# Second attention by four heads at a time: four score banks, one output bank in halves, four buffers of transposed probabilities

## The chip, the core and the metric

The kernel is one program on one NeuronCore of a Trainium2 chip. It has five engines that run side by side and meet through semaphores: PE (TensorE, the matmuls), DVE (VectorE), ACT (ScalarE), POOL (GpSimd) and SP (SyncE, which issues most DMAs). The accumulators of the matmuls lie in PSUM, eight banks of 128 partitions x 512 floats. The metric is the device time of one execution in microseconds (us); lower is better. Times below are us unless marked otherwise.

## The reference, cut to what matters

Two transformer-like blocks follow each other on 256 tokens of width 1024. The change is in the second block. It projects the tokens once (`w_in`), does three attentions, and mixes them by gates:

```python
h = rmsnorm_2(x, norm_mix_pre[l]);  proj = h @ w_in[l]
(q_mb, k_mb, v_mb, q_sw, k_sw, v_sw, q_me, g_mb, g_sw, g_me) = jnp.split(proj, cuts, axis=-1)
o_mb = moba_attention(...)     # 8 heads of 64; 256 tokens are one block: causal, with a bias
o_sw = swa_attention(...)      # 8 heads of 64 on 2 key heads, causal, window of 128, with a sink
o_me = memory_attention(...)   # 4 heads of 128 over 256 memory tokens
merged = (sigmoid(g_mb) * (o_mb @ w_branch_moba) + sigmoid(g_sw) * (o_sw @ w_branch_swa)
          + sigmoid(g_me) * (o_me @ w_branch_mem))
```

A head is scores = q k, exp(scores + bias - max), divided by the row's sum, times v.

## The kernel before, in words

Each engine has its program written out by hand, in one fixed order; the order of the Python text is the order of the queue. Weights come as units of 1 MB. Unit u is loaded into `raw` (four slots), ACT's `split(u)` makes its high part `whi`, DVE's `split(u)` its low part `wlo` (ACT waits until PE is done with the slot), and PE does every product in three matmuls (high x high, high x low, low x high).

Heads are numbered through the program. 0 to 15 are the first block's attention, 16 to 23 are MoBA heads, 24 to 31 sliding window heads (with a sink), 32 to 35 memory heads. "Second attention" here means heads 16 to 31. A head H runs over the engines like this:

- PE `score_pair(p)` (L1425, L1428): scores of heads A = 2p and B = 2p + 1, side by side in the upper and lower 64 rows of the array, into `score_bank`: bank 2 or 3.
- DVE `row_max(H)` (L2056, L2058, for a sink L2064): adds the bias, writes the negated scores to one of the four buffers `prob4`, takes the maximum. It waits for the scores and for the transposes of head H - 4 (`s_pt`), which read the same buffer. It raises `s_Sfree`: the score bank is free.
- ACT `exps(H)` (L919, L921, for a sink L930): exponentials and row sums. Waits for `row_max(H)`.
- DVE `norm_probs(H)` (L2075 to L2079): divides by the sum. Waits for `exps(H)`.
- PE `probs_T(H)` (L1475): three 128 x 128 transposes into `pt_bank`: bank 4 or 5.
- ACT `probs_out(H)` (L939): copies them to one of two buffers `probT2`. Raises `s_ptc`.
- PE `pv_pair(p)` (L1444, L1447): probabilities times values for A and B, into `out_bank`: bank 6 or 7.
- ACT `attn_hi` (L951) and DVE `attn_lo` (L2087): one pair's output as high and low part. The latter raises `s_olo`.

PE's time between these steps is filled with sixteen gate groups, `gate_group(0)` to `gate_group(15)`: 24 matmuls of 128 x 256 each (L1129), two groups to a weight unit. Each is read out by DVE `gate_out2(k)` (L2193) and passed through tanh by ACT `gate_tanh(k)` (L1027). One turn i of the loop (eight turns) holds two heads and two groups. PE does scores of the next pair, PV of the pair before, group 2i, the six transposes of heads A and B, group 2i + 1. DVE does two `row_max` and two `norm_probs` of the next pair, `attn_lo`, `gate_out2(2i)`, a weight split, `gate_out2(2i+1)`. ACT does two `exps` of the next pair, `attn_hi`, a weight split, a tanh, two `probs_out`, a tanh. After the loop come `branch(0, 0)`, 12 matmuls, and the last PV pair, then the other `branch` groups.

Of the kernel before, what the change touches and what calls it, by code (L numbers as in the profile page):

```python
# [7 lines left out]
F32 = mybir.dt.float32  # L8
# [101 lines left out]
def bank_of(g):  # L110

    if g in (G_MLP0, G_MLP0 + 1, G_MLP1, G_MLP1 + 1, G_QMB, G_QMB + 1):
        return 4 + 2 * (g % 2)
    if G_QME <= g < G_QME + 4:
        return (1, 4, 0, 5)[g - G_QME]
    if g in [f + i for f in (G_REC[0], G_FFN) for i in range(2)]:
        return 4 + g % 2
    for b in G_BR:
        if b <= g < b + 8:
            return (1, 0, 2, 3)[(g - b) % 4]  # L120
    return g % 2 if G_G2[0] <= g < G_FFN else g % 4
# [16 lines left out]
def bass_blocks(nc, A, out):  # L138
# [57 lines left out]
    with ctx:  # L196
# [192 lines left out]
        def place_of(H):  # L389

            if H < 32:
                return prob4[:, H % 4, :], probT2[:, H % 2, :], H % 4
# [12 lines left out]

        def out_bank(H):
            return 1 if H < 16 else 6 + out_of(H) % 2

# [198 lines left out]
        def _(act):  # L607
# [325 lines left out]
            def probs_out(H):  # L933
                n = 384 if H < 32 else 512
                act.wait_ge(s_pt, H + 1)
                if H >= 2:

                    act.wait_ge(s_pv, H - 1 if H < 32 else max(H - 1, 32))
                act.activation(place_of(H)[1][:, 0:n], PS[:, pt_bank(H), 0:n], ACT.Copy).then_inc(s_ptc, 1)  # L939

            def attn_hi(H):
                if not ends_out(H):
                    return
                o = out_of(H)
# [6 lines left out]
                act.activation(X[:, k, 0, :], PS[:, out_bank(H), 0:T], ACT.Copy).then_inc(s_ohi, 1)  # L951

# [75 lines left out]

            exps(16)
            exps(17)  # L1030
            for i in range(8):
                A, B = 16 + 2 * i, 17 + 2 * i
                if i < 7:
                    exps(A + 2)
                    exps(B + 2)
                if i:
                    attn_hi(A - 1)
                split(U_G2[i // 4] + i % 4 + LEAD)
                gate_tanh(2 * i)
                probs_out(A)  # L1040
                probs_out(B)
                gate_tanh(2 * i + 1)
            split(U_BR[0] + LEAD)
            attn_hi(31)
            split(U_BR[0] + 1 + LEAD)
# [71 lines left out]
        def _(pe):  # L1117
# [313 lines left out]
            def pv_pair(p):  # L1431

                A, B = 2 * p, 2 * p + 1
                pe.wait_ge(s_ptc, B + 1)
                if p:

                    pe.wait_ge(s_olo, p if p < 8 else p - 1)
                for last in range(2):
                    for H in (A, B):
                        lo, pT = 64 * (H % 2), place_of(H)[1]  # L1440
                        c = 64 * H if H < 16 else 64 * (H - 16) if H < 24 else lo
                        v = (vtok if H < 16 else v_mb if H < 24 else v_sw)[:, last, c:c + 64]
                        if not last:
                            pe.matmul(PS[lo:lo + 64, out_bank(H), 0:T], v, pT[:, 0:T], start=True, stop=False,  # L1444
                                      skip_group_check=True)
                        else:
                            pe.matmul(PS[lo:lo + 64, out_bank(H), P:T], v, pT[:, T:T + P], start=False, stop=True,  # L1447
                                      skip_group_check=True).then_inc(s_pv, 1)
# [131 lines left out]
            ins.then_inc(s_step, 1)  # L1580
            unit_a(U_QKV + 9, G_QME)
            pe.wait_ge(s_evac, G_KSW)
            score_pair(8)
            pe.wait_ge(s_bev, B_VSW + 1)
            unit_a(U_QKV + 10, G_QME + 2)

# [25 lines left out]

            for i in range(8):
                A, B = 16 + 2 * i, 17 + 2 * i
                if i < 7:
                    score_pair(9 + i)
                if i:
                    pv_pair(7 + i)
                gate_group(2 * i)
                if i == 0:  # L1620
                    pe.wait_ge(s_evac, G_QME + 4)
                probs_T(A)
                probs_T(B)
                gate_group(2 * i + 1)

            pe.wait_ge(s_olo, 12)
            branch(0, 0)
            pv_pair(15)
            for k in range(1, 8):
# [88 lines left out]
        def _(dve):  # L1718
# [362 lines left out]
            def attn_lo(H):  # L2081
                if not ends_out(H):
                    return
                o = out_of(H)
                dve.wait_ge(s_ohi, o + 1)
                X, k = attn_dst(o)
                dve.tensor_tensor(X[:, k, 1, :], PS[:, out_bank(H), 0:T], X[:, k, 0, :].bitcast(F32), ALU.subtract)\  # L2087
                   .then_inc(s_olo, 1)
# [115 lines left out]
            dve.wait_ge(s_b2, 2)  # L2204
            row_max(16)
            row_max(17)
# [4 lines left out]
            mem_q_out(1, 1)  # L2211
            split(U_QKV + 10 + LEAD)
            for i in range(8):
                A, B = 16 + 2 * i, 17 + 2 * i
                if i < 7:
                    row_max(A + 2)
                    row_max(B + 2)
                    norm_probs(A + 2)
                    norm_probs(B + 2)
                if i:  # L2220
                    attn_lo(A - 1)
                gate_out2(2 * i)
                split(U_G2[i // 4] + i % 4 + LEAD)
                gate_out2(2 * i + 1)
            branch(0, 0)
            attn_lo(31)
            for k in range(1, 8):
# [135 lines left out]
```

## Time and profile before

| | us |
|---|---|
| median of three runs (1011.65 to 1012.15) | 1011.75 |
| the profiled execution, whole | 1011.99 |
| its span, first to last instruction | 1010.1 |
| PE busy (6251 matmuls) | 996.9 (99%) |
| DVE busy | 699.5 (69%) |
| ACT busy | 546.9 (54%) |
| share of PE in the chain of work that ended last | 92% |

The stage that the change touches starts with the first score pair at 651.46 and ends behind the last PV pair at 724.72. In the timeline a row is `start, duration, engine, line, operation, out<-in, count`; matmuls overlap their successors, and so do the others a little, so that the cost of a step is read from one row's start to the next row's start, not from the duration. A bracket at the end is idle time of the engine and what ended it.

### The profile page before, as it was taken

How to read it: one execution, taken by the hardware profiler on the slowest of the kernel's cores; microseconds unless marked ns; L12 is line 12 of the kernel's file. 1: busy time of each engine (PE TensorE's matmuls, PEld its weight loads, DVE VectorE, ACT ScalarE, POOL GpSimd, SP SyncE). 2: the span in 40 equal slices, each digit the busy share in tenths (PEclk: the TensorE clock that was granted, in tenths of full speed). 3: DMA queues.
4: the chain of work that ended last, by engine and by line, in shares of the span. 5: the costliest groups of instructions: out<-in, count | busy, mean ns of one | idle time of the engine just before them, and what ended most of it. 6: DMA issues, size and time to landing. Idle time of an engine off the chain costs nothing.

```text
span 1010.1 us, 15625 instructions
## 1 busy us (share of the span) xinstructions
PE 996.9 (99%) x6251; PEld 884.8 (88%) x6251; DVE 699.5 (69%) x1000; ACT 546.9 (54%) x803; POOL 84.4 (8%) x102
## 2 busy tenths in 40 slices
PE   9999999999999999999999999999999999999997
PEld 8997888888888867888888899999999899999996
DVE  6989666556567687675756565587665769878785
ACT  7996464444447477654444453366553466555552
POOL 2710010000002210000200000000004200000000
PEclk9999999999999999999999999999999999999999
DMA  9746585656535606575655646354545626565521
GB/s 316 243 154 216 169 314 182 198 178 205 171 121 174 243 1 221 196 248 178 199 176 197 189 139 214 125 168 126 143 150 170 222 81 209 195 198 178 193 100 42
DMA packets 120307, 180.40 MB, mean 179 GB/s; under 512 B 3145, under 2 KB 93609, under 8 KB 120249
## 3 DMA queue, kind: packets, MB, share of 16 engines
q1 hardware_dynamic: 118376, 174.10, 52.8%
q0 software_dynamic: 1536, 5.36, 1.5%
q8 instruction: 41, 0.67, 0.3%
q10 hardware_dynamic: 337, 0.13, 0.0%
q14 instruction: 17, 0.14, 0.0%
HBM read 178.48 MB, written 1.10 MB: 178 GB/s over the span
## 4 chain that ended last, share of the span: by engine, by line
PE 92%; ACT 4%; DVE 3%; issue 1%; POOL 0%; DVEq 0%; POOLq 0%; ACTq 0%
PE PS L1194 28%; PE PS L1129 28%; PE PS L1136 12%; PE PS L1138 6%; PE PS L1353 4%; PE PS L1396 2%; PE PS L1493 2%; PE PS L1182 1%; PE PS L1649 1%; PE PS L1475 1%; PE PS L1263 1%; PE PS L1444 1%; PE PS L1163 1%; PE PS L1238 1%; ACT arena L799 1%
## 5 line engine op out<-in xcount | busy, mean ns | idle before, releaser
L1747 DVE TENSOR_TENSOR wlo<-raw,whi 128x2048 fp32r<-128x2048 f32 x153 | 352.0, 2304 | 112.0 <-ACT whi L636 111.7
L636 ACT ACTIVATE whi<-raw 128x2048 fp32r<-128x2048 f32 x153 | 291.8, 1910 | 139.6 <-PE PS L1194 101.1
L1129 PE MATMUL PS<-XA,whi 128*128 128x256 f32 x1488 | 272.2, 285 | 0.0
L1129 PEld LDWEIGHTS PS<-XA,whi 128*128 128x128 f32 x1488 | 232.6, 192 | 3.0 <-issue 1.9
L1129 PE MATMUL PS<-XA,wlo 128*128 128x256 f32 x744 | 210.4, 283 | 0.0
L1194 PE MATMUL PS<-whi,XB 128*128 128x512 f32 x728 | 207.1, 391 | 1.5 <-DVE wlo L1747 1.4
L1136 PE MATMUL PS<-XA,whi 128*128 128x512 f32 x512 | 182.1, 398 | 0.5 <-DVE XA L1784 0.5
L1194 PEld LDWEIGHTS PS<-whi,XB 128*128 128x128 f32 x728 | 133.9, 188 | 29.8 <-DVE wlo L1747 1.9
L1138 PE MATMUL PS<-XA,wlo 128*128 128x256 f32 x512 | 143.7, 281 | 0.0
L1129 PEld LDWEIGHTS PS<-XA,wlo 128*128 128x128 f32 x744 | 142.5, 192 | 0.0
L1136 PEld LDWEIGHTS PS<-XA,whi 128*128 128x128 f32 x512 | 96.2, 188 | 24.3 <-issue 1.1
L1194 PE MATMUL PS<-wlo,XB 128*128 128x512 f32 x364 | 116.0, 390 | 0.0
L1138 PEld LDWEIGHTS PS<-XA,wlo 128*128 128x128 f32 x512 | 96.7, 189 | 1.1
L1194 PEld LDWEIGHTS PS<-wlo,XB 128*128 128x128 f32 x364 | 68.4, 188 | 14.4
L847 ACT ACTIVATE arena<-PS 128x256 f32<-128x256 f32 x64 | 24.2, 383 | 90.0 <-PE PS L1138 89.9
L1959 DVE TENSOR_TENSOR arena<-PS,arena 128x256 f32<-128x256 f32 x64 | 26.4, 420 | 38.4 <-ACT arena L847 38.4
L1129 PE MATMUL PS<-XB,whi 128*128 128x256 f32 x256 | 46.4, 284 | 0.2 <-issue 0.2
L1094 ACT ACTIVATE arena<-arena,fvec 128x256 f32<-128x256 f32 x44 | 25.6, 596 | 35.5 <-DVE arena L2312 35.5
L1353 PE MATMUL PS<-whi,XA 128*128 128x512 f32 x128 | 42.3, 397 | 0.0
L1129 PEld LDWEIGHTS PS<-XB,whi 128*128 128x128 f32 x256 | 39.9, 192 | 0.5 <-issue 0.5
L2298 DVE SCALAR_TENSOR_TENSOR arena<-arena,fvec 128x256 f32<-128x256 f32 x88 | 38.6, 480 | 1.5 <-ACT arena L1094 0.7
L1194 PE MATMUL PS<-whi,XA 128*128 128x512 f32 x128 | 36.9, 390 | 0.0
(253 smaller groups left out, 1213.5 us busy)
## 6 DMA issues: line engine op xcount, KB each, us to landing
raw<-in_w_up SPq DMA_DIRECT2D x32, 1024.0 KB, 5.5
raw<-in_w_down SPq DMA_DIRECT2D x32, 1024.0 KB, 4.9
raw<-in_w_ffn_up SPq DMA_DIRECT2D x22, 1024.0 KB, 5.1
raw<-in_w_in SPq DMA_DIRECT2D x21, 1024.0 KB, 5.3
raw<-in_w_ffn_down SPq DMA_DIRECT2D x11, 1024.0 KB, 4.9
raw<-in_w_kv SPq DMA_DIRECT2D x8, 1024.0 KB, 5.1
raw<-in_a_w_in SPq DMA_DIRECT2D x7, 1024.0 KB, 8.9
raw<-in_w_mem_kv SPq DMA_DIRECT2D x4, 1024.0 KB, 5.2
```

The costliest lines, as they stand in the source:

```text
L636: act.activation(whi[:, s, :], raw[:, s, :], ACT.Copy).then_inc(s_hi, 1)
L847: act.activation(dst, PS[:, bank_of(g), T:2 * T], ACT.Copy).then_inc(s_low, 1)
L1094: act.activation(fc[:, f, :], fu[:, f, 2:2 + T], ACT.Identity, scale=fvec[:, 1, c:c + 1], bias=fvec[:, 1, 44 + c:45 + c]).then_inc(s_fc, 1)
L1129: ins = pe.matmul(PS[:, bank_of(g), 0:T], w[:, k, P * m:P * m + P], X[:, k0 + k, part, :], start=(i == 0 and part == 0 and w is hi), stop= ...
L1136: pe.matmul(PS[:, bank, :].rearrange("p (e n) -> p e n", e=2), hi, x, start=opens, stop=False, skip_group_check=True)
L1138: return pe.matmul(PS[:, bank, 0:T], lo, x[:, 0, :], start=False, stop=closes, skip_group_check=True)
L1194: return pe.matmul(PS[:, bank + n * t + c, 0:width], X[:, k0 + k, part, P * t:P * t + P], w[:, k, c0 + 512 * c:c0 + 512 * c + width], star ...
L1353: ins = pe.matmul(PS[:, t_banks[t], :], X[:, 4 * i + k, part_, P * t:P * t + P], w[:, k, :], start=(i == 0 and k == 0 and part_ == 0 and w ...
L1396: ins = pe.matmul(PS[:, Q_BANKS[t][c], :], XB[:, 2 * i + k, part_, P * t:P * t + P], w[:, k, 512 * c:512 * c + 512], start=(i == 0 and k = ...
L1747: dve.tensor_tensor(wlo[:, s, :], raw[:, s, :], whi[:, s, :].bitcast(F32), ALU.subtract).then_inc(s_lo, 1)
L1959: dve.tensor_tensor(dst, PS[:, bank_of(g), 0:T], dst, ALU.add).then_inc(s_evac, 1)
L2298: ins = dve.scalar_tensor_tensor(fc[:, f, :], fu[:, f, i:i + T], fvec[:, 0, c:c + 1], fc[:, f, :], ALU.mult, ALU.add)
```

## The change

Heads 16 to 31 now go by four. Score banks are 2, 3, 4, 5 (`H % 4`), transposes all go through bank 6, both PV pairs of a quad share bank 7 in halves of 256 columns, and there are four buffers for the transposed probabilities, two of them new and in free places of the arena (`v_sw` moves for it). A wait moves with each:

```diff
-        return (1, 4, 0, 5)[g - G_QME]
+        return (1, 6, 0, 7)[g - G_QME]
...
-        v_sw = area(S[3] + 1536, 256).rearrange("p (t n) -> p t n", t=TT)
+        probT4 = [probT2[:, 0, :], probT2[:, 1, :], area(S[0] + 1536, 384), area(S[3] + 1536, 384)]
+        v_sw = area(S[3] + 1280, 256).rearrange("p (t n) -> p t n", t=TT)
...
+        def in_quad(H):
+            return 16 <= H < 32
...
-            return 2 + H % 2
+            return 2 + H % (4 if in_quad(H) else 2)
...
-            return 0 if H < 16 else 4 + H % 2
+            return 0 if H < 16 else 6 if in_quad(H) else 4 + H % 2
...
+        def pv_done(H):
+            return H // 4 * 4 + 4 if in_quad(H) else H + 1
```

ACT's waits (`probs_out`, `attn_hi`), and its order:

```diff
-                    act.wait_ge(s_pv, H - 1 if H < 32 else max(H - 1, 32))
+                    act.wait_ge(s_pv, H - 1 if H < 16 else H - 3 if H < 32 else max(H - 1, 32))
...
-                act.wait_ge(s_pv, H + 1)
+                act.wait_ge(s_pv, pv_done(H))
...
+            for e in range(4):
+                exps(16 + e)
+            for q in range(4):
+                H0 = 16 + 4 * q
+                if q:
+                    attn_hi(H0 - 3)
+                    attn_hi(H0 - 1)
+                for e in range(4):
+                    if e % 2 == 0:
+                        i = 2 * q + e // 2
+                        split(U_G2[i // 4] + i % 4 + LEAD)
+                    gate_tanh(4 * q + e)
+                    probs_out(H0 + e)
+                    if q < 3:
+                        exps(H0 + 4 + e)
```

PE's waits (`score_pair`, `pv_pair`, `probs_T`), and its order:

```diff
-                    pe.wait_ge(s_Sfree, A)
+                    pe.wait_ge(s_Sfree, A if A < 16 else A // 4 * 4)
...
-                    pe.wait_ge(s_olo, p if p < 8 else p - 1)
+                    pe.wait_ge(s_olo, p if p < 8 else p // 2 * 2)
...
-                    pe.wait_ge(s_ptc, H if H < 16 else H - 1)
+                    pe.wait_ge(s_ptc, H if H < 32 else H - 1)
...
+            pe.wait_ge(s_bev, B_VSW + 1)
+            for p in (8, 9):
+                score_pair(p)
             unit_a(U_QKV + 10, G_QME + 2)
...
+            for q in range(4):
+                if q < 3:
+                    for p in (10 + 2 * q, 11 + 2 * q):
+                        score_pair(p)
+                if q:
+                    for p in (6 + 2 * q, 7 + 2 * q):
+                        pv_pair(p)
+                for e in range(4):
+                    gate_group(4 * q + e)
+                    if (q, e) == (0, 0):
+                        pe.wait_ge(s_evac, G_QME + 4)
+                    probs_T(16 + 4 * q + e)
 
             pe.wait_ge(s_olo, 12)
             branch(0, 0)
-            pv_pair(15)
+            for p in (14, 15):
+                pv_pair(p)
```

DVE's order:

```diff
+            for q in range(4):
+                H0 = 16 + 4 * q
+                norm_probs(H0 + 3)
+                if q:
+                    attn_lo(H0 - 3)
+                    attn_lo(H0 - 1)
+                for e in range(4):
+                    gate_out2(4 * q + e)
+                    if e % 2 == 0:
+                        i = 2 * q + e // 2
+                        split(U_G2[i // 4] + i % 4 + LEAD)
+                    if q < 3:
+                        if e:
+                            norm_probs(H0 + 3 + e)
+                        row_max(H0 + 4 + e)
```

Three places show what moved. In the changed kernel the same statements stand some 10 lines further down: L1141 is the gate matmul, L1437/L1440 the scores, L1488 the transposes, L1457/L1460 PV; on DVE L2210 is `gate_out2`, L1763 the split, L2072/L2074/L2080 `row_max`, L2091 to L2095 `norm_probs`.

PE, between gate groups 5 and 6 of the program before (turn 3 begins: scores of heads 24 and 25, PV of heads 20 and 21):

```order
L1129 MATMUL PS<-XA,whi 128x256 x2
L1129 MATMUL PS<-XA,wlo 128x256
L1425 MATMUL PS<-arena 128x128 x2
L1428 MATMUL PS<-arena 128x256 x2
L1444 MATMUL PS<-probT,arena 64x256 x2
L1447 MATMUL PS<-probT,arena 64x128 x2
L1129 MATMUL PS<-XA,whi 128x256 x2
```

PE now, behind gate group 7, where quad q = 2 begins (transposes of head 23, scores of heads 28 to 31, PV of heads 20 to 23):

```order
L1141 MATMUL PS<-XA,wlo 128x256
L1488 MATMUL PS<-ident,arena 128x128 x3
L1437 MATMUL PS<-arena 128x128 x2
L1440 MATMUL PS<-arena 128x256 x2
L1437 MATMUL PS<-arena 128x128 x2
L1440 MATMUL PS<-arena 128x256 x2
L1457 MATMUL PS<-probT,arena 64x256 x2
L1460 MATMUL PS<-probT,arena 64x128 x2
L1457 MATMUL PS<-arena 64x256 x2
L1460 MATMUL PS<-arena 64x128 x2
L1141 MATMUL PS<-XA,whi 128x256 x2
```

The scores of the next quad and the PV of the last one stand together, once in four gate groups and not in every second, and directly ahead of them stand the transposes of the quad's last head.

DVE before, in a turn for two heads without a sink (the maximum of the second head, to which that of the first is directly ahead, then both divisions, `attn_lo`, the first gate):

```order
L2056 ISA arena,snmax<-PS,arena 128x128
L2056 ISA snmax 128x1
L2058 ISA arena,snmax<-PS,arena 128x256
L2058 ISA snmax 128x1
L2076 RECIPROCAL srec<-ssum 128x2
L2078 TENSOR_SCALAR arena<-arena,srec 128x128
L2079 TENSOR_SCALAR arena<-arena,srec 128x256
L2076 RECIPROCAL srec<-ssum 128x2
L2078 TENSOR_SCALAR arena<-arena,srec 128x128
L2079 TENSOR_SCALAR arena<-arena,srec 128x256
L2087 TENSOR_TENSOR XB<-PS,XB 128x256
L2193 TENSOR_TENSOR arena<-PS,rstd_row 128x256
```

DVE now, the steps e = 1 and e = 2 in a quad of heads with a sink:

```order
L2210 TENSOR_TENSOR arena<-PS,rstd_row 128x256
L2091 TENSOR_TENSOR ssum<-ssum,ssink 128x2
L2092 RECIPROCAL srec<-ssum 128x2
L2094 TENSOR_SCALAR arena<-arena,srec 128x128
L2095 TENSOR_SCALAR arena<-arena,srec 128x256
L2072 ISA arena,smax<-PS,arena 128x128
L2072 ISA smax 128x1
L2074 ISA arena,smax<-PS,arena 128x256
L2074 ISA smax 128x1
L2080 TENSOR_SCALAR snmax<-smax,nsinks 128x2
L2210 TENSOR_TENSOR arena<-PS,rstd_row 128x256
L1763 TENSOR_TENSOR wlo<-raw,whi 128x2048
```

The division of a head now stands ahead of the maximum of the next head. It waits for the exponentials of its own head, so the maxima no longer run ahead of them.

## Rows read from the trace of the kernel before

**Rows 1.** Busy by engine of the stage: PE, PEld, DVE, ACT, POOL, clock, DMA, GB/s.

```profile
651.46:724.72 73.26, 73.26 (x622) 66.88 (x621) 56.02 (x165) 47.66 (x121) 0.00 (x0) 1.00 0.43 135
```

**Rows 2.** Timeline of PE in the stage, columns as told above.

```profile
651.01 0.40 PE L1129 MATMUL PS<-XA,whi 128*128 128x256 f32 x2
651.25 0.28 PE L1129 MATMUL PS<-XA,wlo 128*128 128x256 f32 x1
651.46 0.49 PE L1425 MATMUL PS<-arena 64*128 64x128 f32 x4
...
652.31 0.50 PE L1129 MATMUL PS<-XA,whi 128*128 128x256 f32 x2
...
662.09 0.82 PE L1475 MATMUL PS<-ident,arena 128*128 128x128 f32 x6
662.66 0.48 PE L1129 MATMUL PS<-XA,whi 128*128 128x256 f32 x2
...
666.55 0.65 PE L1444 MATMUL PS<-probT,arena 128*64 128x256 f32 x4
...
667.35 0.50 PE L1129 MATMUL PS<-XA,whi 128*128 128x256 f32 x2
```

**Rows 3.** Timeline of PE in the first attention: one head's transposes alone.

```profile
361.50 0.49 PE L1475 MATMUL PS<-ident,arena 128*128 128x128 f32 x3
361.75 0.48 PE L1353 MATMUL PS<-whi,XA 128*128 128x512 f32 x1
```

**Rows 4.** Timeline of DVE in the stage.

```profile
652.51 0.29 DVE L2056 CUSTOM_DVE_ANT_0 arena<-PS,arena 128x128 f32<-128x128 f32 x1 [0.52 <-PE PS L1428]
...
653.07 0.29 DVE L2056 CUSTOM_DVE_ANT_0 arena<-PS,arena 128x128 f32<-128x128 f32 x1
...
688.41 2.29 DVE L1747 TENSOR_TENSOR wlo<-raw,whi 128x2048 fp32r<-128x2048 f32 x1 [0.46 <-ACT whi L636]
690.62 0.42 DVE L2193 TENSOR_TENSOR arena<-PS,rstd_row 128x256 f32<-128x256 f32 x1
691.36 0.29 DVE L2056 CUSTOM_DVE_ANT_0 arena<-PS,arena 128x128 f32<-128x128 f32 x1 [0.32 <-PE PS L1428]
...
692.17 0.28 DVE L2056 CUSTOM_DVE_ANT_0 arena<-PS,arena 128x128 f32<-128x128 f32 x1
...
694.57 0.16 DVE L2075 TENSOR_TENSOR ssum<-ssum,ssink 128x2 f32<-128x2 f32 x1
694.77 0.17 DVE L2076 RECIPROCAL srec<-ssum 128x2 f32<-128x2 f32 x1
...
695.43 0.42 DVE L2087 TENSOR_TENSOR XB<-PS,XB 128x256 fp32r<-128x256 f32 x1
```

**Rows 5.** Timeline of ACT in the stage.

```profile
692.30 0.40 ACT L919 ACTIVATE arena<-arena,snmax 128x128 f32<-128x128 f32 x1 [0.81 <-DVE snmax L2064]
...
693.19 0.28 ACT L930 ACTIVATE ssink<-snmax,sinks 128x2 f32<-128x2 f32 x1
693.38 0.39 ACT L919 ACTIVATE arena<-arena,snmax 128x128 f32<-128x128 f32 x1
...
694.71 1.90 ACT L636 ACTIVATE whi<-raw 128x2048 fp32r<-128x2048 f32 x1
696.51 0.40 ACT L1027 ACTIVATE arena<-arena 128x256 f32<-128x256 f32 x1
696.82 0.84 ACT L939 ACTIVATE probT<-PS 128x384 f32<-128x384 f32 x2
```

**Rows 6.** Timeline of PE at the program's start and its last matmul.

```profile
1.52 6.52 PE L1238 MATMUL PS<-ident 128*128 128x128 f32 x30 [1.52 <-POOL ident L496]
...
9.05 0.83 PE L1238 MATMUL PS<-ident 128*128 128x128 f32 x6
...
1003.95 0.39 PE L1194 MATMUL PS<-whi,XB 128*128 128x512 f32 x1
```

**Rows 7.** Busy by engine behind the last matmul, columns as in rows 1.

```profile
1007.50:1008.00 0.50, 0.00 (x0) 0.00 (x0) 0.12 (x1) 0.00 (x0) 0.00 (x0) 0.73 0.36 139
```

More of the change, by code:

```diff
@@ L391, in place_of @@
             if H < 32:
-                return prob4[:, H % 4, :], probT2[:, H % 2, :], H % 4
+                return prob4[:, H % 4, :], probT4[H % (2 if H < 16 else 4)], H % 4
             return prob_me[:, H % 2, :], probT_me[:, H % 2, :], H % 3
@@ L397, in head_of, with out_col @@
             return H % 16 if H < 24 else 8 + (H - 24) // 2 + 4 * (H % 2)
+        def in_quad(H):
+            return 16 <= H < 32
         def score_bank(H):
-            return 2 + H % 2
+            return 2 + H % (4 if in_quad(H) else 2)
         def pt_bank(H):
-            return 0 if H < 16 else 4 + H % 2
+            return 0 if H < 16 else 6 if in_quad(H) else 4 + H % 2
         def out_bank(H):
-            return 1 if H < 16 else 6 + out_of(H) % 2
+            return 1 if H < 16 else 7 if in_quad(H) else 6 + out_of(H) % 2
+        def out_col(H):
+            return T * (H // 2 % 2) if in_quad(H) else 0
+        def pv_done(H):
+            return H // 4 * 4 + 4 if in_quad(H) else H + 1
         FILLS = [[0, 1], [1, 1], [1, 1], [0, 1], [2, 1], [2, 1], [2, 1], [1, 1]]
@@ L950, in attn_hi @@
                         act.wait_ge(s_step, AFTER[U_BR[0] + 1])
-                act.activation(X[:, k, 0, :], PS[:, out_bank(H), 0:T], ACT.Copy).then_inc(s_ohi, 1)
+                act.activation(X[:, k, 0, :], PS[:, out_bank(H), out_col(H):out_col(H) + T], ACT.Copy).then_inc(s_ohi, 1)
             exps(0)
@@ L1027, in gate_tanh @@
                 act.activation(g_br[b][:, k % 8, :], g_br[b][:, k % 8, :], ACT.Tanh, scale=0.5).then_inc(s_tanh, 1)
[L1029 to L1042, printed above, removed]
+            for e in range(4):
[13 more added lines that the diff above has]
+                        exps(H0 + 4 + e)
             split(U_BR[0] + LEAD)
+            attn_hi(29)
             attn_hi(31)
@@ L1442, in pv_pair @@
                         v = (vtok if H < 16 else v_mb if H < 24 else v_sw)[:, last, c:c + 64]
+                        oc = out_col(H)
                         if not last:
-                            pe.matmul(PS[lo:lo + 64, out_bank(H), 0:T], v, pT[:, 0:T], start=True, stop=False,
+                            pe.matmul(PS[lo:lo + 64, out_bank(H), oc:oc + T], v, pT[:, 0:T], start=True, stop=False,
                                       skip_group_check=True)
                         else:
-                            pe.matmul(PS[lo:lo + 64, out_bank(H), P:T], v, pT[:, T:T + P], start=False, stop=True,
+                            pe.matmul(PS[lo:lo + 64, out_bank(H), oc + P:oc + T], v, pT[:, T:T + P], start=False, stop=True,
                                       skip_group_check=True).then_inc(s_pv, 1)
@@ L1580, in _ @@
             ins.then_inc(s_step, 1)
+            pe.wait_ge(s_bev, B_VMB + 1)
             unit_a(U_QKV + 9, G_QME)
             pe.wait_ge(s_evac, G_KSW)
-            score_pair(8)
             pe.wait_ge(s_bev, B_VSW + 1)
+            for p in (8, 9):
+                score_pair(p)
             unit_a(U_QKV + 10, G_QME + 2)
@@ L1611, in gate_group @@
                 group(G_G2[k // 8] + k % 8, u % SLOTS, k % 2, W8, KT, XA)
[L1613 to L1624, printed above, removed]
+            for q in range(4):
[10 more added lines that the diff above has]
+                    probs_T(16 + 4 * q + e)
             pe.wait_ge(s_olo, 12)
             branch(0, 0)
-            pv_pair(15)
+            for p in (14, 15):
+                pv_pair(p)
             for k in range(1, 8):
@@ L2084, in attn_lo @@
                 o = out_of(H)
-                dve.wait_ge(s_ohi, o + 1)
+                dve.wait_ge(s_ohi, o // 2 * 2 + 2 if in_quad(H) else o + 1)
                 X, k = attn_dst(o)
-                dve.tensor_tensor(X[:, k, 1, :], PS[:, out_bank(H), 0:T], X[:, k, 0, :].bitcast(F32), ALU.subtract)\
+                dve.tensor_tensor(X[:, k, 1, :], PS[:, out_bank(H), out_col(H):out_col(H) + T], X[:, k, 0, :].bitcast(F32),
+                                  ALU.subtract)\
                    .then_inc(s_olo, 1)
@@ L2204, in _ @@
             dve.wait_ge(s_b2, 2)
-            row_max(16)
-            row_max(17)
+            for e in range(4):
+                row_max(16 + e)
             split(U_QKV + 9 + LEAD)
@@ L2211, in _ @@
             mem_q_out(1, 1)
+            norm_probs(18)
             split(U_QKV + 10 + LEAD)
[L2213 to L2224, printed above, removed]
+            for q in range(4):
[4 more added lines that the diff above has]
+                    attn_lo(H0 - 1)
+                for e in range(4):
+                    gate_out2(4 * q + e)
[6 more added lines that the diff above has]
+                        row_max(H0 + 4 + e)
             branch(0, 0)
+            attn_lo(29)
             attn_lo(31)
```

## The prediction

> **What bounds the kernel now.** I read the table first: PE is busy for 99% of the span and holds 92% of the chain of work that ended last. Then the stage that is changed, by the view of busy time in a stretch: in its 73.26 us PE is busy for 73.26, DVE for 56.02, ACT for 47.66, and the granted clock is 1.00, the 2.4 GHz level [rows 1]. So there is no wait of PE here that the change could remove. It can win only what PE loses when it goes from one kind of work to another, and it loses every time that PE has to wait.
>
> **Pieces and their lengths** (from the start of a row to the start of the next one):
>
> - PE [rows 2]: two gate matmuls take 0.24 (651.01 to 651.25), so a step is 0.12; the first two behind other work read 0.50 or 0.48 in place of 0.40, a restart of 0.10 or 0.08. A gate group of 24 is 2.88 and the restart, 2.98. A score pair is 0.85 (651.46 to 652.31), a PV pair 0.80 (666.55 to 667.35), six transposes 0.57 (662.09 to 662.66), three alone 0.25 [rows 3]. With the restart that is 0.65 for six and 0.33 for three: to cut them in two costs nothing. Going into a score pair costs another 0.09: by the step it would start at 651.37, it starts at 651.46.
> - DVE [rows 4]: a row maximum 0.56 without a sink (652.51 to 653.07), 0.81 with one; a division 0.86 with a sink (694.57 to 695.43), 0.20 less without; a split 2.21; a gate read-out 0.42, of which some 0.34 till the next can start (my estimate from the overlaps in these rows).
> - ACT [rows 5]: an exponential with a sink 1.08 (692.30 to 693.38), 0.19 less without; a split 1.80; a tanh 0.31; a copy of transposed probabilities 0.42 (two in 0.84).
> - A handover between engines 0.1 to 0.2: the score pair's last matmul gives way at 652.31, DVE starts at 652.51; the maximum of head B ends by 692.17 plus, ACT starts at 692.30 [rows 2, 4, 5].
>
> **What it saves.** Work blocks that stand together pay for going in and out once: 0.09 + 0.10 = 0.19. Before, there are 18 blocks between gate matmuls in the stage: two lone score pairs, six of a score and a PV pair, two lone PV pairs, eight of transposes. By the walk of the new order the 8 score pairs and 8 PV pairs lie in six blocks: 8+9; 10+11; 12+13 with PV 8+9; 14+15 with PV 10+11; PV 12+13; PV 14+15. That is 10 such blocks before and 6 after, 4 x 0.19 = 0.76. The transposes keep their price, whether alone or glued to scores. I take **-0.7**. Bounds: 0 and -1.
>
> **What it adds: three waits of PE.** The new order puts the transposes of a quad's last head directly ahead of the next quad's scores, and these wait until all four maxima of the present quad are done (`s_Sfree` at 24 ahead of pair 12, at 28 ahead of pair 14). But `row_max(23)` waits for the transposes of head 19, which free its buffer: it can't start before PE stands in front of pair 12. And DVE comes to it late. On DVE each maximum now stands behind the division of the head before, which waits for that head's exponentials on ACT, which wait for that head's maximum. Two engines take turns, nothing overlaps, and both weight splits of a quad lie in that line. Walked through for quad q = 1 (heads 24 to 27, with sinks), from the end of gate group 4:
>
> gate read-out 0.2 + 0.34, DVE split 2.20, max 24 0.82, handover and exp 24 0.1 + 1.09, division 24 0.03 + 0.86, max 25 0.82, exp 25 0.1 + 1.09, ACT split 1.81 (it stands ahead of exp 26), DVE split 0.02 + 2.20, division 25 0.86, max 26 0.82, exp 26 0.1 + 1.09, division 26 0.03 + 0.86, max 27 0.82, handover 0.1: sum **16.3**.
>
> PE has in the same time three transposes and three gate groups with theirs: 0.33 + 3 x (2.98 + 0.33) = **10.3**. So PE stands for 6.1 us in this quad (0.4 ahead of the transposes of head 23, since the one bank for transposes is free only when head 22 has been copied, and 5.7 ahead of score pair 14).
>
> Quad q = 0 has the same line without sinks. The gate read-out of group 1 takes part in it, covered by ACT. Four maxima are 0.27 shorter each, three exponentials and three divisions 0.2 shorter each, sum 14.1: PE stands for 14.1 - 10.3 = **3.8** ahead of pair 12. Quad q = 2 has no next scores, but PV pair 13 needs the copy of head 27. `probs_out(27)` stands on ACT behind `exps(30)` and a tanh. The line up to exp 30 is 16.3 - 0.1 - 0.82 - 0.86 - 0.03 = 14.5, plus tanh 0.31, copy 0.42 and a handover of 0.12: 15.4, against 10.3 + 0.80 (PV pair 12) on PE: **4.3**. Sum of the three: 3.8 + 6.1 + 4.3 = **14.2**. It rests on some twenty-five handovers of 0.03 to 0.2, so I give it 1.2 on either side.
>
> Quad q = 3 has no exponentials, nothing waits there. Its cover: PE works 13.2 us (four groups and transposes), DVE 1.4 + 4.4, ACT 1.2 + 1.7 + 3.6. Nor do I expect one in front of the quads: DVE does four maxima instead of two ahead of `mem_q_out(1, 0)`, for which gate group 0 waits, so it comes at some 656.9, and PE gets there at 660.7. The splits are ordered three units (some 19 us) ahead of their use; a delay of 6 us stays inside that, and SP's loads queue behind the splits, not ahead. Nothing of the 14.2 comes back later: behind the stage PE is the bound again.
>
> **The clock.** PE stands still for 3.8, 5.7 and 4.0 us in one piece. What that does the trace shows at its end: the last matmul starts at 1003.95 and takes 0.39 [rows 6], PE does nothing more, and in the half microsecond from 1007.50 the mean clock reads 0.73, falling from 1.00 to 0.50 [rows 7], so at about 1007.7, after 3.4 us of standing. At the program's start 30 records of a 128 x 128 matmul take 6.52, and 6 of the same later 0.83 [rows 6]: 30 at the later pace would be 4.15, so coming up from the low level (1.2 GHz) cost about 2.4 us there. That is the price I take for one fall. The longest wait is well over 3.4 us, the other two little over; I count on the fall in the longest alone. Bounds for this term: 0 and three times 2.4.
>
> The Trainium skill, page "TensorE: Matmul & The Clock Gate", section "HAM oscillation — how this bites in real kernels", tells of a matmul kernel whose waits for data let the clock fall again and again. The rows at this trace's end agree that a standing PE loses its clock; no row here shows what a wait in mid-program does. By that rule all three waits could let it fall, which is rival 2.
>
> **Sum.** Profiled execution: 1011.99 + 14.2 - 0.7 + 2.4 = 1027.9. The median is 0.24 below it: **1027.7**, 1.6% slower.
>
> **Rivals.**
>
> 1. The clock stays up through all waits. For it: in the whole stage before it reads 1.00, and the one fall in these rows comes where PE has ended for good, not where it waits. Against it: two thirds more than those 3.4 us are waited for here. 1011.75 + 14.2 - 0.7 = 1025.3. Chance 0.23.
> 2. It falls in two or three of the waits. All three are longer than the 3.4 that the end of the trace shows, which speaks for it. That the two shorter ones exceed it by only 0.4 to 0.6 speaks against. 1030.1 with two, 1032.5 with three. Chance 0.27.
> 3. DVE and ACT keep pace, and only the buffer's wait stays: three transposes' handover 0.28, one maximum 0.56 or 0.81 and a handover 0.1, once each for pairs 12 and 14, 2.1 together. It needs the line of 16.3 to be under 10.3. 1011.75 - 0.7 + 2.1 = 1013.2. Chance 0.04.
> 4. The other side: the waits are hidden, and merging the blocks decides. The mechanism is PE's entry and exit, 0.19 a block, four times. It decides from the point where the maximum of head 23 (27) is done when PE arrives at pair 12 (14). 1011.75 - 0.7 = 1011.1, no change that can be measured. Against it: that maximum waits for transposes that PE does directly ahead. Chance 0.02. With scores or loads that I overlook it could be a little faster still: 0.01.
>
> **How the numbers follow.** The forecast has a chance of 0.43, rivals 0.23, 0.27, 0.04, 0.03. The range reaches from the first rival less the 1.2 of the handovers, and a little for the savings' bound, to the second rival with two falls and the 1.2, and half way to three: **1023.5 to 1032**. Left out are the rivals 3 and 4 (0.07) and about a third of rival 2 (0.08). Some 0.2% (2 us) is what a measurement of this kernel can tell from no change. Faster by more: 0.01. Within 0.2%: 0.06 (rivals 3 and 4). Slower: 0.93.
>
> **What would show it.** In the changed profile, score pairs (L1437) wait for DVE's maximum (L2074 or L2080) twice, for about 4 and 6 us, and a PV pair (L1457) waits for ACT's copy (L949) once for about 4. The transposes (L1488) wait for L949 by 0.4 twice. PE's busy share in the stage falls from all of it to some 83%. DVE waits for ACT's exponentials before most divisions, ACT for DVE's maxima before most exponentials. If the clock falls, the stretch behind the longest wait reads 0.50 and its gate matmuls take twice as long. The forecast is wrong if the maxima run ahead of the exponentials after all, if the sum of PE's waits is under 10 or over 18, or if the later stages give time back.

## The result, and the profile after

The changed kernel takes **1031.67 us** (median of five runs, 1030.21 to 1031.96) against 1011.75 (1011.63 to 1012.15) of the kernel before on the same chip. The ratio is 1.0193, with an interval of 1.0183 to 1.0204: 1.9% slower. The prediction said 1027.7 with a range of 1023.5 to 1032, so the range held it, by 0.3 at its upper end, and the forecast itself was 4.0 too low.

The page of the profile of after, the span, the first part (busy us, share of the span, instructions), the clock's line of the second part (40 slices of 25.8 us, tenths of full speed), and the chain that ended last by engine:

```profile
span 1030.1 us, 15625 instructions
...
PE 1001.9 (97%) x6251; PEld 889.1 (86%) x6251; DVE 699.2 (68%) x1000; ACT 547.4 (53%) x803; POOL 84.4 (8%) x102
...
PEclk9999999999999999999999999988899999999999
...
PE 84%; DVE 7%; ACT 5%; issue 1%; DMA 1%; SPq 1%; POOL 0%; DVEq 0%; POOLq 0%; ACTq 0%
```

The counts of instructions are those of before and DVE and ACT do the same amount of work, but PE's part of the chain fell from 92% to 84%. DVE and ACT now stand in the chain, and three slices show a lower clock. All three lie where the change is. The stage itself (columns as in [rows 1], which is the same row of before):

```profile
651.24:744.80 93.56, 78.48 (x622) 71.63 (x621) 55.15 (x164) 48.64 (x120) 0.00 (x0) 0.89 0.34 107
```

It starts at 651.24 and its last PV pair gives way to a `branch` matmul at 744.74, so it takes 93.50 in place of 73.26, 20.24 more. The span grew by 20.0. So the whole loss is in the stage, and the 285 us behind it give nothing back. PE's busy share in it is 84%, against 100% before.

What PE waits for between 640 and 760 in after, from the view of waits (engine, bank, line waited at, what ended it: us in total, times, longest):

```profile
PE PS L1437 <- DVE smax L2074: 5.4, 1, 5.4
PE PS L1437 <- DVE snmax L2074: 4.4, 1, 4.4
PE PS L1457 <- ACT arena L949: 3.8, 1, 3.8
PE PS L1488 <- ACT arena L949: 1.4, 2, 0.7
```

These are the waits forecast, at the places forecast: the scores wait for DVE's maximum twice, PV pair 13 waits once for ACT's copy, and the transposes twice, briefly, for the copy of the head before. With the 5.4 and the 0.7 ahead of it, the second quad costs the most, as worked out. (The 0.7 at the transposes had been forecast as 0.4.)

The clock, from PE's timeline in after (start, duration, ... and in brackets the idle time ahead of it):

```profile
672.81 0.49 PE L1488 MATMUL PS<-ident,arena 128*128 128x128 f32 x3
...
677.70 0.80 PE L1437 MATMUL PS<-arena 64*128 64x128 f32 x4 [4.41 <-DVE snmax L2074]
678.29 1.06 PE L1440 MATMUL PS<-arena 64*128 64x256 f32 x4
...
686.08 0.49 PE L1488 MATMUL PS<-ident,arena 128*128 128x128 f32 x3
...
702.51 0.80 PE L1437 MATMUL PS<-arena 64*128 64x128 f32 x4 [5.44 <-DVE smax L2074]
...
721.84 0.39 PE L1460 MATMUL PS<-probT,arena 128*64 128x128 f32 x4
...
726.03 1.12 PE L1457 MATMUL PS<-arena 128*64 128x256 f32 x4 [3.80 <-ACT arena L949]
```

and from the view of stretches, around the first and the third wait (columns as in [rows 1]; the granted clock is the number behind POOL's):

```profile
675.50:676.00 0.50, 0.00 (x0) 0.00 (x0) 0.13 (x1) 0.50 (x3) 0.00 (x0) 0.98 0.18 53
676.00:676.50 0.50, 0.00 (x0) 0.00 (x0) 0.15 (x1) 0.50 (x3) 0.00 (x0) 0.50 0.87 311
...
677.00:683.00 6.00, 5.30 (x32) 3.64 (x32) 1.36 (x8) 0.98 (x4) 0.00 (x0) 0.52 0.27 105
...
723.50:724.00 0.50, 0.00 (x0) 0.00 (x0) 0.46 (x4) 0.00 (x0) 0.00 (x0) 0.77 0.58 90
```

PE's last matmul ahead of the first wait ends at 673.3, and at 676.0 the clock drops to the 1.2 GHz level. PE resumes at 677.70; the mean of 0.52 from 677 to 683 puts the return to 2.4 GHz at some 682.8. The rows of score matmuls show what that means: `64x256 x4` takes 1.06, where before it took 0.60. The same slow rows follow both other waits. At the third, PE's last matmul ends at 722.23 (721.84 + 0.39) and the mean of 0.77 from 723.50 puts the fall at some 723.8, after only 1.5 us of standing. The clock fell three times, not once.

Of the serial line that makes these waits, here are steps of the quad that I walked through, q = 1. DVE in after:

```profile
688.81 0.28 DVE L2072 CUSTOM_DVE_ANT_0 arena<-PS,arena 128x128 f32<-128x128 f32 x1
...
690.96 0.16 DVE L2091 TENSOR_TENSOR ssum<-ssum,ssink 128x2 f32<-128x2 f32 x1 [0.92 <-ACT ssink L940]
...
691.82 0.28 DVE L2072 CUSTOM_DVE_ANT_0 arena<-PS,arena 128x128 f32<-128x128 f32 x1
...
695.76 2.29 DVE L1763 TENSOR_TENSOR wlo<-raw,whi 128x2048 fp32r<-128x2048 f32 x1 [2.65 <-ACT whi L646]
```

and ACT:

```profile
692.75 0.40 ACT L929 ACTIVATE arena<-arena,snmax 128x128 f32<-128x128 f32 x1 [1.14 <-DVE snmax L2080]
...
693.83 1.90 ACT L646 ACTIVATE whi<-raw 128x2048 fp32r<-128x2048 f32 x1
...
699.76 0.40 ACT L929 ACTIVATE arena<-arena,snmax 128x128 f32<-128x128 f32 x1 [3.35 <-DVE snmax L2080]
```

They read as one sentence: maximum 24 (688.81), DVE idle 0.92 till ACT's exponential is done, division (690.96), maximum 25 (691.82), ACT idle 1.14 till then, exponential (692.75), ACT's split (693.83), DVE idle 2.65 until it is done, DVE's split (695.76), and only then the next division and maximum, for which ACT idles 3.35. Each of the two engines is busy for far less than the stage's 93.5 us (DVE 55.2, ACT 48.6), but they take turns, and one of them stands at nearly every step.

### The profile page after: what moved, and what is told of

Read it like the earlier page. It is cut to its first block, busy times and chain, and to the rows that moved or that the text cites. A ratio compares the mean times of both kernels' runs of the same rounds, so it can differ in the third digit from the quotient of the medians.

```text
span 1030.1 us, 15625 instructions
## 1 busy us (share of the span) xinstructions
PE 1001.9 (97%) x6251; PEld 889.1 (86%) x6251; DVE 699.2 (68%) x1000; ACT 547.4 (53%) x803; POOL 84.4 (8%) x102
## 4 chain that ended last, share of the span: by engine, by line
PE 84%; DVE 7%; ACT 5%; issue 1%; DMA 1%; SPq 1%; POOL 0%; DVEq 0%; POOLq 0%; ACTq 0%
PE PS L1206 28%; PE PS L1141 23%; PE PS L1148 12%; PE PS L1150 6%; PE PS L1365 4%; DVE wlo L1763 3%; PE PS L1408 2%; PE PS L1506 2%; ACT whi L646 1%; PE PS L1194 1%; PE PS L1665 1%; DMA raw<-in_a_w_in 1%; PE PS L1457 1%; ACT arena L931 1%; PE PS L1440 1%
## 5 line engine op out<-in xcount | busy, mean ns | idle before, releaser
L1763 DVE TENSOR_TENSOR wlo<-raw,whi 128x2048 fp32r<-128x2048 f32 x153 | 352.1, 2305 | 115.2 <-ACT whi L646 114.9
L1141 PE MATMUL PS<-XA,whi 128*128 128x256 f32 x1488 | 273.5, 286 | 0.0
L1141 PEld LDWEIGHTS PS<-XA,whi 128*128 128x128 f32 x1488 | 233.9, 193 | 2.4 <-issue 1.3
L1141 PE MATMUL PS<-XA,wlo 128*128 128x256 f32 x744 | 211.0, 284 | 0.0
L1141 PEld LDWEIGHTS PS<-XA,wlo 128*128 128x128 f32 x744 | 143.2, 193 | 0.0
L1141 PE MATMUL PS<-XB,whi 128*128 128x256 f32 x256 | 46.5, 284 | 0.2 <-issue 0.2
L1141 PEld LDWEIGHTS PS<-XB,whi 128*128 128x128 f32 x256 | 39.8, 192 | 0.5 <-issue 0.5
```

Source lines behind the costliest of these rows:

```text
L1141: ins = pe.matmul(PS[:, bank_of(g), 0:T], w[:, k, P * m:P * m + P], X[:, k0 + k, part, :], start=(i == 0 and part == 0 and w is hi), stop= ...
L1763: dve.tensor_tensor(wlo[:, s, :], raw[:, s, :], whi[:, s, :].bitcast(F32), ALU.subtract).then_inc(s_lo, 1)
```

## The experiments

Each kernel was compared with the kernel before on the same chip; the ratio's 95% interval stands in parentheses. All the edits are made to the changed kernel.

**1. Is it the clock?** PE does idle matmuls on a constant (L1250, the kernel's own `keep_warm`) inside the three waits, into a bank that is free there. They compute nothing that is used. The waits ahead of them keep that bank free, and everything else is as in the changed kernel.

```diff
             for q in range(4):
+                if q in (1, 2):
+                    pe.wait_ge(s_olo, 8 if q == 1 else 10)
+                    keep_warm((18, 22)[q - 1], 7)
                 if q < 3:
...
+                        if p == 13:
+                            pe.wait_ge(s_Sfree, 29)
+                            keep_warm(14, 2)
                         pv_pair(p)
```

> The changed kernel, with 18, 22 and 14 idle matmuls of the identity (about 0.22 us each, into a free bank) directly ahead of the three long waits of PE, shorter than the waits (4.7, 5.7 and 3.9 us from step to step). Theory A (the waits cost their length, and the clock that falls in them about 2 us each on top): the clock stays at 1.00 in the stage, PE still stands in front of the same pairs for some 0.7 to 0.8 us each, and the time is 1031.7 less 6.0, that is 1025.7. Theory B (DVE and ACT set the pace in the whole stage, so that PE at half speed behind a wait costs nothing): the clock stays up too, but the time stays within 1 us of 1031.7. Theory C (the extra time beyond the waits is something else of the quads, such as banks that two engines share): 1031.7 as well, with the clock up.

Measured: 1025.64 (1025.34 to 1025.9), ratio 1.0137 (1.0120 to 1.0154). That is 6.0 below the changed kernel. One burst in e1's timeline of PE, and the score matmuls behind it:

```profile
672.99 4.18 PE L1250 MATMUL PS<-ident 128*128 128x128 f32 x36
677.56 0.49 PE L1437 MATMUL PS<-arena 64*128 64x128 f32 x4 [0.39 <-DVE snmax L2080]
677.88 0.60 PE L1440 MATMUL PS<-arena 64*128 64x256 f32 x4
...
683.49 0.49 PE L1488 MATMUL PS<-ident,arena 128*128 128x128 f32 x3
```

PE starts the scores as late as in the changed kernel (677.56 against 677.70), but a row of four of them takes 0.60 and not 1.06. From 640 to 760 the clock reads 1.00:

```profile
640.00:760.00 120.00, 116.99 (x988) 111.26 (x987) 73.58 (x196) 59.86 (x143) 0.00 (x0) 1.00 0.43 131
```

So the 20 us are two things. Some 6.0 is clock, 2.0 a fall. The remaining 14 us is standing still, which no warm clock gives back. The two traces give the price of each fall: from the start of the scores to the next transposes PE takes 8.38 in the changed kernel (677.70 to 686.08) and 5.93 here (677.56 to 683.49), 2.45 more. Behind the second and the third wait the same comparison gives 1.98 and 2.02, 6.5 in all, as the two spans differ by 6.6.

**2. Is it the weight splits in the serial line?** The second split of each quad goes behind the last exponential (ACT) and the last maximum (DVE). In the kernel after it stood ahead of the third.

```diff
-                    if e % 2 == 0:
-                        i = 2 * q + e // 2
-                        split(U_G2[i // 4] + i % 4 + LEAD)
+                    if e == 0:
+                        split(U_G2[q // 2] + 2 * q % 4 + LEAD)
...
+                    if e == 3:
+                        split(U_G2[q // 2] + 2 * q % 4 + 1 + LEAD)
```

> The changed kernel, only the second weight split of each quad moved on ACT and on DVE from step e = 2 to the end of step e = 3, behind the last exponential and the last maximum. Theory A (ACT and DVE take turns in one serial line, and both splits lie in it): the line loses 1.80 + 2.21 = 4.0 us a quad. Walked through with the measured pieces, PE waits 1.7 ahead of pair 12, 3.1 ahead of pair 14, 1.7 ahead of PV pair 13 and, new, 2.3 ahead of the transposes of head 29, which a split on ACT now delays; 8.7 together in place of 16.0. At most one of them is long enough for the clock to fall. Time 1018 to 1021. Rival (the splits are covered by the waits of either engine for the other, and the order of maximum and division alone makes the line): within 2 us of 1031.7.

Measured: 1019.25 (1017.86 to 1019.56), ratio 1.0068 (1.0052 to 1.0085). PE's waits in e2, 640 to 760:

```profile
PE PS L1438 <- DVE smax L2075: 2.5, 1, 2.5
PE PS L1489 <- ACT probT L949: 2.1, 1, 2.1
PE PS L1438 <- DVE snmax L2075: 1.4, 1, 1.4
PE PS L1458 <- ACT arena L949: 0.7, 1, 0.7
```

6.7 are left of 15.0. In the second quad the scores' 5.4 and the transposes' 0.7 became 2.5 in all: DVE reads out the gate at 682.16 and PE starts the scores at 694.38, a line of 12.2 in place of 16.2 (686.27 to 702.51 in the changed kernel), shorter by both parts of the split (1.81 and 2.20 in my walk). The 2.1 at transposes (L1489, 722.67) is new and was expected: it is the price of the moved split. The late split of quad 2 and the first of quad 3 now follow each other closely on ACT (715.62 and 717.95), DVE's gate read-out (721.28) stands behind its own late split, and only then come the tanh and the copy for which PE waits. The clock fell once, around the 2.5, and not at the 2.1:

```profile
694.00:696.00 2.00, 1.62 (x10) 1.45 (x12) 0.55 (x3) 1.38 (x6) 0.00 (x0) 0.57 0.00 0
```

**3. Is it the order of division and maximum?** On DVE the maximum of the next head goes ahead of the division of the head before; the splits stay.

```diff
                     if q < 3:
+                        row_max(H0 + 4 + e)
                         if e:
                             norm_probs(H0 + 3 + e)
-                        row_max(H0 + 4 + e)
```

> The changed kernel, only DVE's two statements of a step swapped: the maximum of head H0+4+e ahead of the division of head H0+3+e. Theory A (one serial line, because each maximum stands behind a division that waits for an exponential): maxima run ahead, PE waits 2.5 ahead of pair 12, 3.8 ahead of pair 14, 3.2 ahead of PV pair 13, together 9.5. The clock falls in one or two. Time 1020 to 1023.5. Rival (the line is set by the splits and gate read-outs, the division's place is of no weight): 1030 to 1032.

Measured: 1022.09 (1021.05 to 1023.83), ratio 1.0098 (1.0081 to 1.0114). PE's waits in e3:

```profile
PE PS L1437 <- DVE smax L2074: 3.2, 1, 3.2
PE PS L1457 <- ACT arena L949: 2.7, 1, 2.7
PE PS L1437 <- DVE snmax L2074: 2.1, 1, 2.1
```

The time was in the band, but in part for a wrong reason: the waits shrank to 8.0, more than I had counted on, and the clock fell three times, where I had expected one or two. It fell even around the wait of 2.1:

```profile
675.00:676.00 1.00, 0.66 (x6) 0.67 (x8) 0.91 (x5) 1.00 (x5) 0.00 (x0) 0.79 0.98 342
```

**4. Both orders at once.** Edits 2 and 3 together.

> The changed kernel with both edits, late second splits and maxima first; PE's order as in the changed kernel, so the transposes of a quad's last head still stand directly ahead of the next scores. Theory A: what stays is the seam itself (the last maximum of a quad can't start before these transposes), 1.0 ahead of pair 12, 1.3 ahead of pair 14, 0.6 ahead of PV pair 13, and 1.2 at head 29 behind a split on ACT; 4.1 together, the clock never falls. Time 1011.75 - 1.8 + 4.1 = 1014.0. Rival (the two orders overlap in what they give and some 4 us of serial line remain): 1018.

Measured: 1013.27 (1013.1 to 1014.79, ten runs), ratio 1.0016 (1.0006 to 1.0026). PE's waits in e4:

```profile
PE PS L1489 <- ACT probT L949: 1.1, 1, 1.1
PE PS L1438 <- DVE smax L2075: 0.8, 1, 0.8
PE PS L1438 <- DVE snmax L2075: 0.8, 1, 0.8
```

The two orders on DVE and ACT carry 18.4 of the 19.9 us, and 1.5 is left. PE's waits of 2.9 (the three here and one of 0.2) are more than that: the quads themselves are a little faster than the pairs of before. The scores still wait 0.8 twice. This is the part of the wait that the buffers make (rival 3 in the prediction, 0.28 + 0.56 or 0.81 + 0.1 = 0.9 to 1.2 each). The 1.1 is the moved split's, as in experiment 2. The time came out 0.7 under what was expected, as the waits and the saving were each a little better.

**5. The seam taken away too.** On PE the next quad's scores and the last quad's PV go one step further, behind the transposes of the quad's first head, and so one gate group and that head's transposes (3.20 together) lie between the transposes of a quad's last head and the scores that wait for it. On DVE the maximum goes first. The splits go where a walk of each engine's queue left room, and the two output parts (`attn_hi`, `attn_lo`) go one step later, which the cut below leaves out.

```diff
-                if q < 3:
-                    for p in (10 + 2 * q, 11 + 2 * q):
+                if q == 0:
+                    for p in (10, 11):
                         score_pair(p)
-                if q:
-                    for p in (6 + 2 * q, 7 + 2 * q):
-                        pv_pair(p)
...
                     probs_T(16 + 4 * q + e)
+                    if q and e == 0:
+                        if q < 3:
+                            for p in (10 + 2 * q, 11 + 2 * q):
+                                score_pair(p)
+                        for p in (6 + 2 * q, 7 + 2 * q):
+                            pv_pair(p)
```

```diff
+            SPLITS = {(0, 0): 0, (0, 3): 1, (1, 0): 2, (1, 3): 3, (2, 0): 4, (3, 0): 5, (3, 1): 6, (3, 3): 7}
...
+                    i = SPLITS.get((q, e))
+                    late = q < 3 and e == 3
+                    if i is not None and not late:
+                        split(U_G2[i // 4] + i % 4 + LEAD)
+                    if q < 3 and e:
+                        norm_probs(H0 + 3 + e)
+                    if i is not None and late:
+                        split(U_G2[i // 4] + i % 4 + LEAD)
```

> The changed kernel with the quad's scores and PV moved on PE by one gate group and one head's transposes (behind the transposes of the quad's first head, not ahead of its first gate group), maxima ahead of divisions, one weight split at the head of each quad and one at its end (in the last quad at its steps 0, 1 and 3), high and low output parts one step later. Theory A (PE's waits are all that the quads cost, and glued blocks give back 1.8 us): the walk with the measured pieces leaves no wait of PE in the stage, the clock stays up, time 1011.75 - 1.8 = 1010.0, ratio 0.998, faster than the kernel before. Rival 1 (the one transposition bank and its copy on ACT still make PE wait by 1 to 2 us in all): 1011 to 1012, no change that can be measured. Rival 2 (the 1.8 us is not there, it is an artefact of my accounts): 1011.8 with no waits.

Measured: **1009.71** (1009.48 to 1009.98, nine runs) against 1012.2 (1011.6 to 1012.78) of before, ratio 0.9975 (0.9965 to 0.9985). That is 22 us under the changed kernel and a quarter of a per cent faster than the kernel before. The stage in e5:

```profile
640.00:760.00 120.00, 119.83 (x1003) 114.55 (x1002) 82.73 (x214) 68.22 (x157) 0.00 (x0) 1.00 0.48 144
```

PE waits nowhere in the stage (the 0.17 in this row, at 733.20, lies behind it and is there in the kernel before too). Where the gain comes from stands in e5's timeline of PE:

```profile
666.60 0.49 PE L1492 MATMUL PS<-ident,arena 128*128 128x128 f32 x3
...
676.62 0.49 PE L1441 MATMUL PS<-arena 64*128 64x128 f32 x4
...
677.38 0.39 PE L1441 MATMUL PS<-arena 64*128 64x128 f32 x4
...
678.13 0.65 PE L1461 MATMUL PS<-probT,arena 128*64 128x256 f32 x4
...
678.83 0.60 PE L1461 MATMUL PS<-arena 128*64 128x256 f32 x4
...
679.58 0.51 PE L1145 MATMUL PS<-XA,whi 128*128 128x256 f32 x2
...
682.56 0.49 PE L1492 MATMUL PS<-ident,arena 128*128 128x128 f32 x3
```

From the transposes of one head to those of the fourth head after it (666.60 to 682.56) is 15.96. Before, two turns, the same work, start at 662.09 [rows 2] and end where the six transposes of the next but one turn begin, in the timeline of PE of before:

```profile
678.55 0.82 PE L1475 MATMUL PS<-ident,arena 128*128 128x128 f32 x6
```

16.46, so a quad is 0.50 cheaper. In the glued block a score pair costs 0.76 or 0.75, where one alone costs 0.85, and a PV pair 0.70 or 0.75, where one costs 0.80. The stage of e5 goes from 651.44 to 722.69, 71.25, or 2.01 less than before; the span is 2.0 shorter.

**6. Only PE's part of experiment 5.** DVE and ACT keep the changed kernel's orders.

> The changed kernel, only PE's order edited: scores of the next quad and PV of the last one behind the transposes of the quad's first head, one gate group later. DVE and ACT keep the changed kernel's order. Theory A (the serial line of DVE and ACT is the bound, not the place of the seam): PE's waits are some 13 us, now in a dozen pieces of 0.3 to 2.0 ahead of the transposes, which wait for copies on ACT; the clock stays up in most of them. Time 1023 to 1026. Rival (the seam itself is the cost: scores stood directly behind the transposes that free their maximum's buffer): waits of under 4 us, 1014.

Measured: 1023.47 (1022.35 to 1024.06), ratio 1.0109 (1.0094 to 1.0125). PE's waits in e6:

```profile
PE PS L1488 <- ACT arena L949: 6.5, 4, 1.8
PE PS L1488 <- ACT probT L949: 2.5, 4, 1.0
PE PS L1488 <- DVE arena L2098: 1.0, 1, 1.0
PE PS L1437 <- DVE smax L2077: 0.2, 1, 0.2
```

The scores no longer wait, as the shift should bring about, except for one 0.2. But 10.2 us of waits in all (some 13 were expected) come in ten small pieces, nine of them at the transposes, which need the same slow line's results one head at a time. The shift alone mends the place where PE stood and not the cause. The clock fell once, behind the second of two equal waits:

```profile
698.54 0.52 PE L1488 MATMUL PS<-ident,arena 128*128 128x128 f32 x3 [1.82 <-ACT arena L949]
...
720.05 0.52 PE L1488 MATMUL PS<-ident,arena 128*128 128x128 f32 x3 [1.82 <-ACT arena L949]
```

```profile
722.00:724.00 2.00, 2.00 (x11) 1.67 (x9) 1.68 (x7) 1.75 (x5) 0.00 (x0) 0.50 0.00 0
```

Behind 698.54 it stayed at 1.00 (698 to 706).

One account for all of them, in us of the profiled executions, against experiment 5 (span 1008.1), in which PE never waits in the stage.

A wait is counted by steps here: from where PE would have gone on at the pace of experiment 5's rows to where it did (in experiment 1 with the idle matmuls in it), which is a little more than the idle time in the brackets. A fall is priced as under experiment 1, by how much longer PE takes from there to the next transposes; single falls come to 1.5 to 2.7. The start is that of the stage, less experiment 5's 651.44.

| kernel | span, less 1008.1 | waits | falls | start | sum |
|---|---|---|---|---|---|
| after | 22.0 | 15.7 | 6.5 (three) | -0.2 | 22.0 |
| 1, idle matmuls | 15.4 | 15.8 | 0 | -0.3 | 15.4 |
| 2, late split | 9.7 | 7.2 | 1.5 (one) | +0.9 | 9.6 |
| 3, maximum first | 13.9 | 8.4 | 5.9 (three) | -0.3 | 13.9 |
| 4, both orders | 3.4 | 3.5 | 0 | -0.2 | 3.4 |
| 6, shift only | 13.4 | 12.0 | 1.5 (one) | -0.1 | 13.4 |

(The sums are taken before rounding. The profiled execution of experiment 3 was its slowest; its median is 1.7 lower.) Waits and falls of the clock make up the whole of each difference to within 0.1, and the rest, experiment 5 against before, is the 2.0 of the glued blocks.

## Why the prediction was right, and where it was off

**What bounds it, and no wait to win:** right. With PE at 100% of the stage before [rows 1], the best arrangement found wins 2.0 us, and from merged blocks alone.

**The three waits, +14.2:** right in place, number and order. By steps they came to 4.5, 5.5 and 4.0, and 0.9 twice at the transposes: 15.7, or 15.0 as idle time. (The 4.7, 5.7 and 3.9 in experiment 1's expectation count from the end of three lone transposes, 0.25; glued to scores they take 0.42, 676.20 to 676.62 in experiment 5.) By steps the bound of 1.2 was passed by 0.3. Two terms were mis-sized. PE's own path I took as 10.3 for a quad: I added the restart of 0.08 to the transposes (0.33) and a restart again to the group (2.98). Measured it is 3.20 a step (663.20 to 666.40 in after), and 10.0 with the last transposes, 0.2 to 0.3 shorter. The serial line I had as 14.1 and 16.3 (its terms add up to 16.36); measured it is 14.5 for q = 0 (663.20 to 677.70) and 16.4 for q = 1 (686.08 to 702.51). The line of twenty-five handovers was within 0.4.

**The cause:** confirmed by experiments 2 to 5. The prediction put it down to two things in one line, the division ahead of the maximum and both splits. Mending one leaves 7.4 or 10.3 us, both leave 1.5. What is left in experiment 4 is 1.8 by steps at the seam between PE's transposes and scores and 1.7 elsewhere, mostly the moved split, less the 2.0 of the glued blocks. Experiment 5 removed both at once, by the shift and by other places for the splits; no run tells what each did alone.

**The saving, -0.7:** right in sign, too small; it is 2.0 in after (93.5 less 15.7 and 6.5 is 71.3) and in experiment 5, outside my bound of -1. I counted only one way in and out per merged block. What I left out is that each pair inside a block is shorter too: 0.75 for 0.85 at scores, as experiment 5's rows show. In the trace of before a score pair followed by PV takes the same 0.86 (673.93 to 674.79) as one alone, so I took this for its price anywhere. I never had two score pairs in a row in the trace, and should have kept the bound wider for it.

**The clock, +2.4:** the price was nearly right, 2.0 to 2.2 a fall in this kernel (6.0 for three by the medians, 6.5 by the traces), and the count was wrong: three falls, not one. This is the step that failed, and it is the largest of the three errors: +4.1 here by the traces, +1.5 at the waits, -1.3 at the saving, 4.3 together, less 0.2 for a stage that began sooner, against the 4.0 of the profiled executions. I let the end of the trace decide, where the clock fell after 3.4 us of standing [rows 7], and took the waits of 4 us as little over that. One event, behind another kind of work, was made a threshold; in after the clock fell 2.7, 2.8 and 1.5 us after the last matmul's end at the three waits. Rival 2 named this outcome with 0.27 in all, for two falls or three; with three it gave 1032.5, and 1031.67 was measured.

That 1032.5 lay outside the range. The range held because the three falls cost 0.7 less than rival 2 would have had them and the larger saving nearly made up for the longer waits: that part is luck. The Trainium skill, page "TensorE: Matmul & The Clock Gate", section "HAM oscillation — how this bites in real kernels", says that a kernel that waits between short bursts pays for the change of clock each time anew. This case's trace agrees: 6.0 us for three waits. I had cited this and then weighed it below a single row.

**Nothing comes back later, nothing in front:** right. The span's 20.0 are the stage's 20.2.

**The rivals:** 1 (clock stays up, 1025.3) fell with the profile; experiment 1 built it, and got 1025.64. 3 (only the buffer's wait) is near experiment 4 in its mechanism: 1013.2 forecast for a kernel in which DVE and ACT keep pace, 1013.27 measured. Both agreements are closer than the terms deserve. In experiment 1 waits longer by 1.6 met a saving larger by 1.3. In experiment 4 the waits were 3.5 by steps and not 2.1, with only 1.8 of them the buffer's, and the saving 2.0 and not 0.7. 4 (waits hidden, merging decides; 1011.1) is experiment 5, where the gain was larger than the 0.7 worked out for it.

## What to carry to other kernels

When work is grouped into larger batches, write down the queue of each in-order engine for one batch and look for a consumer placed ahead of the next producer: here one swapped pair of calls on DVE and a split in the wrong spot made a line of 16 us beside 10 us of PE work, though neither DVE (55.2 us busy) nor ACT (48.6) was near the stage's length. Put what waits for another engine behind what that engine needs next, and leave one piece of independent work between the last release of a buffer and the step that needs it. Price a wait of PE of the sizes that lost the clock here (1.8 us and more) as the wait plus, at worst, a fall of the clock (1.5 to 2.7 us here), each time; grouping by itself is worth only what PE loses between kinds of matmul, a quarter of a per cent here.

## What the runs showed of the hardware that I had not expected

- The clock fell in or behind waits of 5.4, 4.4, 3.8, 3.2, 2.7, 2.5, 2.1 and one of 1.8 us; it stayed up at 2.1 and 1.4 (experiment 2), at another of 1.8 and two of 1.4 (experiment 6), and at all of up to 1.1 (experiment 4). Between 1.8 and 2.1 the length of a wait doesn't tell. What else decides was not tried.
- How long PE had stood when the clock fell differs as well: 2.7, 2.8 and 1.5 us after the last matmul's end in after, 3.4 at the end of the trace of before. The fall behind the 1.8 of experiment 6 came at some 721.5, when PE had been at work again for 1.4 us.
- After a fall the low level holds on for 5.1, 4.2 and 4.6 us after PE resumes (677.70 to 682.8, 702.51 to 706.7, 726.03 to 730.6 in after). The three falls cost 2.45, 1.98 and 2.02 (experiment 1), a little less than half of those stretches.
- Idle matmuls of 128 x 128 in a wait kept the clock at 1.00 with gaps of 0.4 to 0.5 us left (experiment 1). The 0.60 that this kept for a row of four score matmuls was 1.06 without it.
